# Even and odd layers: mixing, routing and experts in one block, and the last expert pair written out behind the loop

## What the kernel computes

```python
x = x + mix
h = rms_norm_2(x, norm_ffn_g[layer])
x = x + hier_moe(h, w_group, b_group, w_expert, b_expert, w_gate, w_up, w_down)
# hier_moe: the best of 4 groups, then the best 2 of its 8 experts (32 experts in all);
#   gates = p(group) * p(expert), renormalised over the two
#   of every expert: (silu(xb @ w_gate[e]) * (xb @ w_up[e])) @ w_down[e], scaled by its gate,
#   and added back to the tokens that chose it
```

## Time and profile before

| | before |
|---|---|
| runs shown, us | 1655.58, 1665.26, 1666.5 |
| profiled execution, us | 1665.39 |
| its span, us | 1663.6 |
| TensorE busy | 1381.3 us, 83% |
| VectorE / ScalarE / GpSimd busy | 379.7 / 277.5 / 96.1 us |
| read from HBM | 494.06 MB |
| mean DMA rate over the span | 299 GB/s |
| mean granted clock of TensorE | 0.922 of 2.4 GHz |

### The profile page before, as it was taken

How to read it: one execution, slowest core, us unless ns; L and a number is a source line. 1 busy time by engine, 2 the same in 40 slices (tenths; PEclk the granted TensorE clock), 3 DMA queues, 4 the chain that set the end, 5 groups by cost and what they waited for, 6 DMA issues and landing times. The chain is left out here.

```text
span 1663.6 us, 21736 instructions
## 1 busy us (share of the span) xinstructions
PE 1381.3 (83%) x9272; PEld 725.0 (44%) x9272; DVE 379.7 (23%) x733; ACT 277.5 (17%) x534; POOL 96.1 (6%) x98
## 2 busy tenths in 40 slices
PE   7999999997999979676676766898998767867876
PEld 3754456544869554232232322655543322323332
DVE  2331332323555531011010100165411100001010
ACT  1131310322412110210000000113311110101010
POOL 0000000000000006294000000000000000000000
PEclk9999999998999989889898998899989988888789
DMA  9822543245330379999999999744569999999997
GB/s 373 281 86 101 189 165 126 77 151 207 121 129 20 138 318 379 428 429 429 429 429 429 429 429 428 305 153 159 213 281 381 429 429 429 429 429 429 429 429 310
DMA packets 41945, 497.00 MB, mean 299 GB/s; under 512 B 6432, under 2 KB 9248, under 8 KB 11552
## 3 DMA queue, kind: packets, MB, share of 16 engines
q1 hardware_dynamic: 41888, 496.17, 72.6%
HBM read 494.06 MB, written 2.10 MB: 298 GB/s over the span
## 5 line engine op out<-in xcount | busy, mean ns | idle before, releaser
L2595 PE MATMUL banks<-weight_ring,arena 128*32 128x512 f32 x1920 | 294.0, 747 | 178.6 <-DMA weight_ring<-in_moe_weights 171.2
L2595 PEld LDWEIGHTS banks<-weight_ring,arena 128*32 128x32 f32 x1920 | 58.6, 124 | 397.1 <-DMA weight_ring<-in_moe_weights 277.6
L2557 DVE TENSOR_TENSOR arena<-arena,banks 64x512 f32<-64x512 f32 x32 | 22.1, 690 | 669.4 <-ACT arena L2515 669.4
L814 PE MATMUL banks<-weight_ring,hT 128*128 128x512 f32 x384 | 170.1, 600 | 1.5 <-DMA weight_ring<-in_ring_weights 1.5
L2584 PEld LDWEIGHTS banks<-arena,x_normed 128*128 128x128 f32 x1088 | 134.5, 205 | 42.1 <-issue 38.7
L2584 PE MATMUL banks<-arena,x_normed 128*128 128x64 f32 x1088 | 139.3, 290 | 3.0 <-DVE arena L2543 3.0
L2606 PE MATMUL banks<-weight_ring,arena 128*32 128x512 f32 x1024 | 130.0, 645 | 7.9 <-DMA weight_ring<-in_moe_weights 7.9
L322 PE MATMUL banks<-weight_ring,hT 128*128 128x512 f32 x256 | 113.6, 599 | 0.0
L814 PEld LDWEIGHTS banks<-weight_ring,hT 128*128 128x128 f32 x384 | 73.1, 193 | 88.4 <-issue 86.3
L2515 ACT ACTIVATE arena<-banks 64x512 f32<-64x512 f32 x32 | 18.9, 591 | 518.9 <-PE banks L2595 518.9
L2634 PE MATMUL banks<-arena 64*128 64x512 f32 x256 | 63.6, 611 | 25.6 <-ACT arena L2521 25.6
(11 more groups left out here) (489 smaller groups left out, 1336.6 us busy)
## 6 DMA issues: line engine op xcount, KB each, us to landing
weight_ring<-in_moe_weights SPq DMA_DIRECT2D x184, 2048.0 KB, 25.8
weight_ring<-in_ring_weights SPq DMA_DIRECT2D x36, 2048.0 KB, 8.4
arena<-in_moe_weights SPq DMA_DIRECT2D x4, 2048.0 KB, 9.5
weight_ring<-in_ring_weights SPq DMA_DIRECT2D x4, 1024.0 KB, 4.9
mix<-in_moe_weights SPq DMA_DIRECT2D x2, 2048.0 KB, 16.2
hT<-in_moe_weights SPq DMA_DIRECT2D x2, 1024.0 KB, 9.7
arena<-in_moe_weights SPq DMA_DIRECT2D x2, 1024.0 KB, 12.3
arena<-in_c_even SPq DMA_DIRECT2D x1, 1440.0 KB, 6.2
```

Source lines behind the costliest of these rows:

```text
L814: ins = pe.matmul(bank, g.hT[:, k, half * P:(half + 1) * P], w[:, k, :], start=(k == 0), stop=(k == KT - 1))
L2557: dve.tensor_tensor(hid[0:2 * CAP, :], sil[0:2 * CAP, :], b_gu[2 * CAP:4 * CAP, :], ALU.mult).then_inc(s_h, 1)
L2595: ins = pe.matmul(b_gu[q:q + CAP, :], xg[:, 2 * quarter + k, e * CAP:(e + 1) * CAP], up_w(where, quarter, e)[:, which, k, :], start=(quart ...
```

## The change

The expert functions of a layer are no longer a block of their own: `expert_functions` returns one function for each engine, and the mixer's block calls them at the end of its own streams (`moe.sync(sp)`, `moe.scalar(act)`, `moe.vector(dve)`, `moe.tensor(pe)`, and `moe.gpsimd(pool)` in the even layer). The barrier between routing and experts is gone. With it come new orders inside: VectorE writes `rankm` first, then picks, and does shares, gates and number of passes behind the first pick; the gather goes into two banks and is scaled out in two parts; the number of passes is read later; the zero matmuls that open and close the sum banks are gone (the first pair opens them, each sum matmul counts a semaphore of its bank); the transposes of `Pg` stand before the gather; and the last pair is written out behind the loop, without a gather. The core of the diff:

```diff
@@ even_layer (odd_layer likewise, without gpsimd)
+    moe = Experts(g, 0, c0 + 7, router)
...
             router.exps(act)
+            moe.scalar(act)
...
-            router.prepare(dve)
...
             router.select(dve)
-            router.gates(dve)
+            moe.vector(dve)
...
             router.ranks(pe)
-    g.end_phase(router.sems)
-    return c0 + 7, router
+            moe.tensor(pe)
+    g.end_phase()
+    return c0 + 7
@@ Router.select
         self.scale_x(dve, 1)
+        dve.wait_ge(self.s_sel, 1)
+        dve.wait_ge(self.s_rk, 1)
+        pr = ps[4][:, 64:64 + TT * NE].rearrange("p (a n) -> p a n", a=TT)
+        link(dve, dve.scalar_tensor_tensor(out=self.rankm, in0=pr, scalar=1.0, in1=sel, op0=ALU.add, op1=ALU.mult))
+
+    def shares(self, dve):
...
@@ Router.ranks
-        pe.wait_ge(self.s_zero, 2)
-        pe.wait_ge(self.s_x, 4)
-        for b in range(4):
-            ins = pe.matmul(ps[b][:, :], self.zeros[:, 0:P], self.zeros, start=True, stop=False)
-        ins.then_inc(self.s_Pt, 1)
         pe.wait_ge(self.s_xT, 4)
-        self.keep_clock(pe, 6)
+        self.keep_clock(pe, 20)
...
-        self.keep_clock(pe, 10)
+        self.keep_clock(pe, 5)
@@ expert_functions, sync
         for j in range(4, 6):
             released(j - 4, 0, 1)
             load(1, 1, j)
...
+        T = turns(sp)
+        with sp.Fori(0, T) as t:
@@ expert_functions, scalar
             act.activation(sil[0:2 * CAP, :], b_gu[0:2 * CAP, :], ACT.Silu).then_inc(s_sl, 1)
+            act.wait_ge(s_Pt, n + 1)
+            act.copy(PT, b_t[:, S:2 * S]).then_inc(s_PTc, 1)
             act.wait_ge(s_ht, n + 1)
             act.copy(hidT, b_t[:, 0:8 * CAP].rearrange("p (f j) -> p f j", f=4)).then_inc(s_hc, 1)
...
+                of_pair(n)
+                if n == 0:
+                    s5_exps(act)
@@ expert_functions, vector
+        def advance(n, of_next):
+            hidden(n)
+            gathered(n + 1)
+            dve.wait_ge(s_Pt, n + 1)
+            gated(of_next, n + 1)
+
+        pick(0)
+        router.largest(dve)
+        router.shares(dve)
+        gathered(0)
+        router.gates(dve)
+        gated(0, 0)
+        pick(1)
+        router.count_turns(dve)
...
+        if ly == 0:
+            s5_of_vector(dve)
+        T = turns(dve)
...
+            dve.wait_ge(s_sum[j], T * NP)
+            dve.tensor_tensor(v, v, ps[j][:, :], ALU.add).then_inc(s_add, 1)
@@ expert_functions, tensor
+        def of_pair(n, group, opens=False):
+            for quarter in range(4):
+                if quarter % 2 == 0:
+                    pe.wait_ge(s_xg, n * 2 + (quarter // 2 + 1))
+                gate_up(quarter, group, n + 1)
+            pe.wait_ge(s_P, n * 2 + 2)
...  # transposes of Pg
+            gather(n + 1)
...  # transposes of the hidden values
+            pe.wait_ge(s_xg, n * 2 + 4)
+            pe.wait_ge(s_hc, n + 1)
+            down(0, group, n + 1).then_inc(s_da, 1)
+            down(1, group, n + 1).then_inc(s_dn, 1)
+            pe.wait_ge(s_yc, n + 1)
...
+                    pe.matmul(ps[2 * tt + nh][:, :], PT[r, tt * P:(tt + 1) * P], y[r, :], start=opens, stop=True,
+                              skip_group_check=True).then_inc(s_sum[2 * tt + nh], 1)
...  # of_last: the same without the gather; one 128x1 matmul counts s_G in its place
+        gather(0)
+        of_pair(0, 0, opens=True)
+        of_pair(1, 1)
+        T = turns(pe)
+        with pe.Fori(0, T * NP - 3) as i:
+            of_pair(i + 2, 2)
+        of_last(T * NP)
```

More of the change, by code:

```diff
@@ L2361, in select, with largest, count_turns @@
         link(dve, dve.tensor_tensor(c2(316), c2(314), c2(320), ALU.mult))
[L2362 to L2367, removed]
+    def largest(self, dve):
+        self.g.dve_steps.mark(dve.tensor_reduce(self.g.small[:, 330:331], self.g.ps[4][:, 128:128 + NE], AX.X, ALU.max))
+    def count_turns(self, dve):
+        g, sm, link = self.g, self.g.small, self.g.dve_steps.link
         more = S // CAP - 1
@@ L2645, in moe_layer, with gpsimd, sync, released @@
-    g.end_phase()
+    def gpsimd(pool):
+        s5_of_pool(pool)
+    def sync(sp):
+        def released(j, n, more):
+            sp.wait_ge(*((s_gu, n * 4 + (more * 4 + j - 3)) if j < 4 else ((s_da, s_dn)[j - 4], n + more)))
+        def load(group, pair, j):
+            for part, dst in enumerate(at_pair[group][j]):
+                n = dst.shape[1]
+                sp.dma_start(dst, A["moe_weights"][ly, pair, j][:, part * n:(part + 1) * n]).then_inc(landed[group][j], 16)
+        for j in range(4, 6):
+            released(j - 4, 0, 1)
+            load(1, 1, j)
+        for j in range(SLOTS):
+            released((2, 3, 4, 5, 4, 5)[j], 0, 1 if j < 4 else 2)
+            load(2, 2, j)
+        if ly == 0:
+            for dst, name in ((g.s5.B[:, 0], "s5_b"), (g.s5.C[0], "s5_c"), (g.s5.bT, "s5_bT")):
+                sp.dma_start(dst, A[name]).then_inc(g.s5_bc_landed, 16)
+        T = turns(sp)
+        with sp.Fori(0, T) as t:
+            with sp.Fori(0, NP - 3) as i:
+                for j in range(SLOTS):
+                    released(j, t * NP + i, 3)
+                    load(2, i + 3, j)
+            with sp.If(t < T - 1):
+                for pair in range(3):
+                    for j in range(SLOTS):
+                        released(j, t * NP, pair + NP)
+                        load(2, pair, j)
+        g.limit = len(g.chunks)
+        if c0 < g.limit:
+            for j in range(SLOTS):
+                sp.wait_ge(*((s_gu, T * NP * 4) if j < 4 else ((s_da, s_dn)[j - 4], T * NP)))
+                g.send(sp, c0 + j + 1)
+        else:
+            for j in range(4):
+                at = (slice(None), j // 2, slice((j % 2) * 512, (j % 2 + 1) * 512))
+                sp.wait_ge(s_add, j + 1)
+                sp.dma_start(g.out[0].rearrange("(a p) n -> p a n", p=P)[at], g.x[at]).then_inc(g.out_written, 16)
+            sp.wait_ge(g.out_written, 64)
```

341 lines of the change are left out of this document (156 added, 185 removed).

## The result

| | before | after |
|---|---|---|
| median, us (four runs each) | 1665.88 (1655.58 to 1671.1) | 1637.1 (1636.72 to 1644.07) |
| ratio | | 0.9832 (0.9802 to 0.9863) |
| profiled execution, its span, us | 1665.39, 1663.6 | 1636.72, 1634.9 |
| mean granted clock | 0.922 | 0.928 |

The change makes the kernel 1.7% faster. The two spans differ by 28.7 us where 17.65 were forecast.

A forecast was written before the change was run, and what follows sets the result against it. It took full-rate DMA of expert weights as the bound, so earlier starts count. 9.2 + 4.7 + 1.8 + 3.85 - 1.6 - 0.3 = 17.65 us off 1665.39 gave 1647.7 us, range 1639 to 1656.

The forecast's parts named there:

- What bounds the kernel: Stretches of full DMA in both layers, 785 us: only bytes count there, so gains come from starting them earlier.
- Both starts: From ranks to first quarters: quarters begin earlier by 9.2 us in the even layer, 4.7 us in the odd.
- The rival in which the head start doesn't arrive: Even layer's start: odd parameters or something behind them hold pairs 0 and 1; 1656 us, chance 0.08.
- Clock in the first quarters: First 64 quarter records of each layer: closing idle time lifts the clock, 1.8 us for both layers, the middle.
- Pairs 0 and 1: 0: First two pairs: `Pg` transposes move ahead of the gather but stay in the same TensorE series up to the halves; 0.
- Opening the sums ... both end before the selection does: 0: Ahead of the ranks: zero-opening and 6 `keep_clock` calls become 20 calls, both over before the selection ends; 0.
- End: End of both layers: half 1 sooner by 0.65 and 0.4 us, additions by 1.4 us each; together 3.85 us.
- clock and fetch terms: Losses in the last pair, both layers together: 1.6 us for lower clock, 0.3 us for late code fetches.
- late fetches: Last pair's code behind the loop: nothing, or one fetch of some 1 us in a layer; 0.3 us for both.
- The rule that spoke against the change: Half-rate clock in short bursts: first quarters gain nothing, last pair pays 2.5 us in each layer; 1653 us.
- clock good everywhere: Rival: first quarters at 7.07 us in both layers, last pair's bursts at 1.92 us; 1644.1 us, chance 0.2.

The follow-up runs named there:

- e10: Kernel before with two 128x128 matmuls more in each pair and 16 instead of 10 `keep_clock` calls behind the ranks: 1659.04 us, ratio 0.997.
- e7: e2 with 14 instead of 5 `keep_clock` matmuls behind the ranks, filling TensorE's pause: 1641.65 us, ratio 0.9867.
- e1: Changed kernel with the `Pg` transposes and ScalarE's copies moved back between hidden transposes and halves: 1637.68 us, ratio 0.9866.
- e9: Changed kernel with the last pair in the loop, with its gather, and additions waiting for all four sums: 1640.92 us, ratio 0.9861.
- e8: The changed kernel again, unchanged, as a reference: 1637.94 us, ratio 0.983.
- e3: Kernel before with two 128x128 matmuls more in each pair, in TensorE's wait for ScalarE's copy: 1662.02 us, ratio 0.9997.
- e11: Changed kernel with extra matmuls ahead of each pair's halves, between the last pair's halves and before the odd layer's norm: 1635.32 us, ratio 0.9829.
- e2: Changed kernel with VectorE's shares, number of passes and gates ahead of the first pick again: 1650.01 us, ratio 0.9942.

## Why the prediction was right and where it failed

- **What bounds the kernel: right.** Stretches of full DMA keep their length; pair 2 to the last quarter takes 385.47 and 385.22 us in the even layer, 381.33 and 381.66 in the odd one. What starts pair 2 earlier ends the layer earlier.
- **Both starts: right** (9.2 and 4.7 forecast, 9.4 and 4.9 found). The even number depends on the execution: in the kernel before, the quarters wait for the odd parameters and stood 11.70 to 14.48 us behind the ranks in its three profiles, so the same change would have shown 6.7 in one of them. By the quarters' start from the start of the span, 607.28 and 599.04, it is 8.2 us. The rival in which the head start doesn't arrive is refuted: the odd parameters still come after 600 us, but nothing of pairs 0 and 1 waits for them, and the DMA engines go on without a pause.
- **"Clock in the first quarters", 1.8 us: failed by size.** The quarters fell from 8.98 and 8.66 to 7.07 us, 3.5 us: the upper of the two bounds, and I took the middle. They take 7.07 in both layers of all seven profiles without a pause around the first gather, and 8.0 to 9.0 in every start with one, but for e10's odd layer. The gather, named as the evidence against, does not lower the clock by itself: e7 and the changed kernel have it at 3.68 or 3.79 us and 7.07 us for the quarters behind it.
- **"Pairs 0 and 1: 0": failed, and this is the largest term.** The four halves fell from 5.31, 5.34, 5.03 and 5.27 us to 3.64, together 6.4 us. Another 1.5 us came off the rest of the four pairs, 1.0 of it by e1's 0.25 us a pair (the shorter gather, 3.68 for 3.79, is within it); 0.5 is not assigned. The forecast had seen the 5.34 us of the earlier trace rows and read them as belonging to the gather, which stays. Part of the 6.4 us is chance of this pair of profiles: nine of twelve halves are slow in the kernel before, six of 28 in the new form. This pair of profiles has four and none; by the shares 2.1 of four fewer would be slow, about 3.5 us by an estimate from these counts and 1.65 us a slow half. So some 3 us of the 6.4 are luck. Two lines of the timeline before that stand nowhere above, and one of the timeline after:

```profile
621.41 5.31 PE L2606 MATMUL banks<-weight_ring,arena 128*32 128x512 f32 x32
1252.96 5.27 PE L2606 MATMUL banks<-weight_ring,arena 128*32 128x512 f32 x32
...
1226.74 3.64 PE L2649 MATMUL banks<-weight_ring,arena 128*32 128x512 f32 x32 [0.51 <-issue]
```

- **"Opening the sums ... both end before the selection does: 0": failed in the odd layer.** The opening matmuls, at the low clock, held the ranks back to 1208.11 us, 1.26 behind the end of the selection, where the changed kernel needs 0.08 us. That is 1.2 of the 2.5 us ahead of the odd layer's ranks. The other 1.3 us lie ahead of the selection: 0.7 in the norm's transposes (L307, 3.67 us before and 2.96 after), 0.2 in the first projection (16.21 and 15.99), the rest not assigned. Their cause was not tried. Over the profiles the stretch takes 154.0 to 155.3 us in five of kernels of the old form and 150.0 to 153.8 in nine of the new one, and the first projection 16.15 to 16.33 us in those five, 14.08 in six of the nine.
- **End: near.** 1.95 us forecast with the clock and fetch terms, 1.6 found in the ledger, 3.0 by e9's medians. The parts differ: the additions behind the sums' start gave 1.2 us in each layer (1.4 forecast), while the way from the last quarter to the sums gained nothing (13.05 and 13.06 us in the odd layer, 12.80 and 13.04 in the even one). The last pair does lose clock, as forecast: half 0 takes 3.64 us, but it is over before half 1's data land; only the 0.7 us of half 1 count. The 0.3 us for late fetches is a term that no run shows: TensorE's waits in the last pair are for a landing or another engine, but for 0.51 us ahead of half 0, which every pair has.
- **The rule that spoke against the change.** The Trainium skill ("TensorE: Matmul & The Clock Gate", Part 1) has short bursts between waits fall back to the half rate. In the last pair this case's trace agrees (16 records in 3.64 us), though not every execution: in e8's even layer the same half takes 1.92 us. For the first quarters the prediction applied it the wrong way: the change took away the wait that made them such a burst. The rival "clock good everywhere" came nearest with 1644.1 us, still 7 us above the median, since it too left the halves of pairs 0 and 1 as they were.

In sum, of the 11 us that the forecast was short, 7.9 lie in pairs 0 and 1 outside the first quarters, 1.7 in the quarters, 2.5 ahead of the odd ranks and 0.5 in the starts; against them stand 1.2 ahead of the even ranks and 0.3 at the ends.

**Open:** why the halves of pairs 0 and 1 are so often slow in the kernel before. The order inside a pair is one difference, and e1, which has the old order without the pauses, showed one slow half of four, too few to tell. A wait stands ahead of them in both kernels: 0.51 us directly ahead of the halves in the changed one, 0.55 us with two transposes behind it in the one before. With matmuls in that wait the kernel before had no slow half in eight (e3, e10, against nine of twelve); the changed kernel's none in four (e11) are too few beside 6 of 28. That the pauses of the start reach this far, some 20 us on, is not shown: e2 had them and no slow half.

## What to carry to other kernels

A pause ahead of a chain of dependent matmuls can cost more than its length: in e2 a start later by 2.3 us cost 5.6 us in a layer by the rows (6.4 by the medians), because the gather and the first quarters then ran at the lower clock and everything behind them hung on that chain. When a change takes such a pause away, look up in the trace of before which rows of the chain take longer than the same rows elsewhere, and put all of the difference into the upper end of the range, not half of it. Take more than one profile of the kernel before: the same row can run at either clock from one execution to the next. And where a pause can't be taken away, matmuls without use in it can bring back most of the loss (8.4 of 12.8 us in e7 by the medians).

## What the hardware showed that was not expected

- A row of light matmuls (32 records of 64 columns) takes 3.68 to 3.79 us behind other work and 5.64 and 6.07 behind 2.04 us of idle time; the clock then stays low into the 64 records behind it (8.48 and 8.03 us against 7.07). Behind 1.44 to 1.61 us it took 3.79 us in five of ten cases and 5.04 to 5.21 in the other five. The gather of the next pair is at the full rate again in every profile, and the halves behind it are or are not, from one execution to the next.
- Behind a wait of 0.55 us and two transposes, 32 records took 4.93 to 5.34 us instead of 3.64 in nine of twelve cases; with two 128x128 matmuls in the wait, in none of eight. Directly behind a wait of 0.51 us, in the changed kernel, they did so in six of 28.
- The merged block saves the barrier between routing and experts: VectorE's 1.35 and 1.44 us in the earlier trace rows are gone. No idle time that looks like a late fetch is seen where the written-out last pair begins.
